# One stage in place of five: input projection, latent up-projections, rotation and bias tables of a two-layer model on one core

## The reference, cut to what matters

```
h = rmsnorm(x, g_attn_norm)                         # 1024 x 1024
proj = h @ w_in                                     # 1024 x 1952
q_a, k_a, v_a, c_q, c_kv, k_rope = split(proj)      # 512, 512, 512, 256, 128, 32 columns
q  = rmsnorm(c_q, g_q_latent) @ w_q_up              # 256 -> 8 heads x (64 + 32)
kv = rmsnorm(c_kv, g_kv_latent) @ w_kv_up           # 128 -> 8 heads x (64 + 64): k_nope, v
q_rope, k_r = apply_rope(q[..., 64:]), apply_rope(k_rope)
bias = rel_bias[bucket(key_pos - query_pos)]        # per head, plus the dilation's log count
```

## Time and profile before

| | us |
|---|---|
| three executions | 5008.50, 5026.09, 5024.47 |
| their median | 5024.47 |
| the profiled execution, its own time | 5014.29 |
| span of its profile | 5012.5 |
| TensorE busy in the span | 4419.9 (88%) |
| VectorE, ScalarE, GpSimd busy | 1840.9, 1680.9, 1239.1 |

### The profile page before, as it was taken

One profiled execution on the slowest core, in us unless ns is written; L12 is line 12 of the kernel. 1 busy time (PEld: TensorE's weight loads), 2 busy tenths in 40 slices (PEclk: granted clock), 3 DMA queues, 4 the chain that ended last, 5 costly groups with the idle time before them and its releaser, 6 DMA issues. The chain is left out here.

```text
span 5012.5 us, 60867 instructions
## 1 busy us (share of the span) xinstructions
PE 4419.9 (88%) x23843; PEld 3654.4 (73%) x23843; DVE 1840.9 (37%) x3384; ACT 1680.9 (34%) x2691; POOL 1239.1 (25%) x646
## 2 busy tenths in 40 slices
PE   7838999767699759999969999949989999999998
PEld 6625999757344347778759999849978877888886
DVE  2122665422111133323136665765522424200154
ACT  2123544310011054553235555534432324211132
POOL 4112322121100023232122332431054211222242
PEclk9966999875799979999979999979989999999999
DMA  3154311233699762232221111121065312322243
GB/s 123 61 159 134 91 43 43 77 120 120 223 325 322 259 217 84 74 102 78 90 84 36 39 52 39 65 68 35 26 225 170 118 59 92 111 74 66 96 152 114
DMA packets 391530, 559.54 MB, mean 112 GB/s; under 512 B 104507, under 2 KB 257723, under 8 KB 389947
## 3 DMA queue, kind: packets, MB, share of 16 engines
q1 hardware_dynamic: 362604, 474.27, 30.1%
q10 hardware_dynamic: 19280, 49.04, 2.5%
q0 software_dynamic: 9376, 32.52, 1.8%
HBM read 402.35 MB, written 153.40 MB: 111 GB/s over the span
## 5 line engine op out<-in xcount | busy, mean ns | idle before, releaser
L2949 POOL TENSOR_TENSOR end_w_lo<-end_w_raw,end_w_hi 128x1024 fp32r<-128x1024 f32 x144 | 353.5, 2463 | 836.0 <-ACT end_w_hi L3138 835.9
L3381 PE MATMUL end_ps<-end_xT_hi,end_w_hi 128*128 128x512 f32 (+1 forms) x896 | 344.7, 385 | 4.7 <-DVE end_xT_lo L2978 2.4
L3381 PE MATMUL end_ps<-end_xT_lo,end_w_hi 128*128 128x512 f32 (+1 forms) x896 | 342.9, 383 | 0.0
L3381 PE MATMUL end_ps<-end_xT_hi,end_w_lo 128*128 128x512 f32 (+1 forms) x896 | 342.8, 383 | 0.0
L1290 PE MATMUL exp_gu_ps<-exp_wgu,exp_xbT 128*128 128x512 f32 x544 | 258.8, 631 | 52.7 <-DMA exp_wgu<-in_w_up 40.4
L2361 POOL TENSOR_TENSOR mid_w_lo<-mid_w_raw,mid_w_hi 128x1024 fp32r<-128x1024 f32 (+1 forms) x64 | 154.2, 2413 | 408.8 <-ACT mid_w_hi L2507 408.8
L662 PE MATMUL att_o_ps<-att_v,att_pT 128*128 128x64 f32 x2048 | 242.6, 272 | 0.0
L1290 PEld LDWEIGHTS exp_gu_ps<-exp_wgu,exp_xbT 128*128 128x128 f32 x544 | 106.9, 202 | 183.3 <-issue 137.6
L3138 ACT ACTIVATE end_w_hi<-end_w_raw 128x1024 fp32r<-128x1024 f32 x144 | 150.0, 1054 | 268.8 <-PE end_ps L3381 139.0
L662 PEld LDWEIGHTS att_o_ps<-att_v,att_pT 128*128 128x128 f32 x2048 | 238.7, 192 | 0.0
L2661 PE MATMUL mid_ps<-mid_w_hi,mid_xT_hi 128*128 128x512 f32 x576 | 229.3, 398 | 6.2 <-DVE mid_xT_lo L2421 6.2
(11 more groups left out here) (576 smaller groups left out, 10450.5 us busy)
## 6 DMA issues: line engine op xcount, KB each, us to landing
exp_wgu<-in_w_gate SPq DMA_DIRECT2D x34, 1024.0 KB, 9.1
exp_wgu<-in_w_up SPq DMA_DIRECT2D x34, 1024.0 KB, 11.6
exp_wd<-in_w_down SPq DMA_DIRECT2D x34, 1024.0 KB, 6.0
mid_w_raw<-in_w_in SPq DMA_DIRECT2D x60, 512.0 KB, 4.0
end_w_raw<-in_w_ffn_in SPq DMA_DIRECT2D x88, 256.0 KB, 3.2
end_w_raw<-in_w_ffn_out SPq DMA_DIRECT2D x44, 512.0 KB, 3.7
expert_rows<-exp_out SPq DMA_DIRECT2D x34, 512.0 KB, 6.3
in_tail<-mid_y SPq DMA_DIRECT2D x56, 256.0 KB, 2.0
```

Of the source, the lines that this page charges most:

```text
L2949: pool.tensor_tensor(halves(w_lo, piece), w_raw[:, 2 * q:2 * q + 2], halves(w_hi, piece).bitcast(F32), ALU.subtract).then_inc(w_split, 1)
L3381: ins = pe.matmul(o_, lhsT, rhs, start=(k == 0 and part == 0), stop=(k == KC - 1 and part == 2))
```

## The change

The five stages become one, `front_layers` "front". What it computes and what the attention reads is the same; q_a, k_a, the table and the latent heads lie in DRAM as before, and v is kept in two tensors of its own (`v_a`, `v_b`).

- The latent columns (chunk "l", 416 columns) are projected first, group by group as the x tiles are turned. The results stay on the chip (`yl`), where ScalarE and VectorE norm them.
- The gains of the norms are folded into the weights as they are split. Weights come in 16 pieces of two K tiles, double-buffered; ScalarE makes the high and VectorE the low parts. GpSimd does nothing but two memsets.
- Then come 24 positions, one group of v, q or k each. Three positions take one latent tile along: its three turns at the first, the product with w_q_up before the second's group and that with w_kv_up in the middle of it, then the rotation, and four batches of four head turns between the halves of the groups that follow. Each batch goes through one PSUM bank and is copied out by ScalarE or VectorE.
- The bias row of all eight heads is made once, by four matmuls of 33 x 8 at the start, and written to DRAM as 8 x 2048. From position 4 on a load spreads one head's row over 128 partitions, and at the next position a store writes it to `skew`.
- Every load and store is issued by SyncE, in one order written out by hand. Groups have two PSUM banks and two buffers of 128 x 512.
- The weights of the up-projections are loaded once all x tiles are turned (their place is that of the x tiles) and split after the last latent tile is kept.

The diff, cut to its core (the bodies of the removed functions are in the section on the kernel before; added lines are moved to the left by eight columns):

```diff
--- before.py
+++ after.py
-def toeplitz_tables(nc, name, rel_bias, onehot_dram, tables, heads, scale):
...
-def head_prep(nc, name, ident_dram, x, kv, dims, cos, sin, outs, gain=None):
...
+FRONT_PLAN = ("l", "v", "q", "k")
+def front_layers(nc, name, a, ident_dram, v_rows, qkT, lat_v, lat_qkT, bias_rows, skew):
...
+    POSITIONS = GROUPS - NT
+    BATCH = 2 * B_HEADS // 4
...
+        def load_piece(n):
+            c, q = divmod(n, PIECES)
+            at, wid = columns(c)
+            if n < 2:
+                sp.wait_ge(hot_done, 4)
+            else:
+                sp.wait_ge(w_split, 2 * (n - 1))
+            src = a["w_in"][2 * q * P:(2 * q + 2) * P, at:at + wid].rearrange("(k p) n -> p k n", p=P)
+            sp.dma_start(w_raw[:, n % 2, :, 0:wid], src).then_inc(w_in[n % 2], 16)
...
+        def load_up():
+            sp.wait_ge(turned, NT)
+            sp.dma_start(raw_q, a["w_q_up"].rearrange("(k p) n -> p k n", p=P)).then_inc(up_in, 16)
+            sp.dma_start(raw_k, a["w_kv_up"]).then_inc(up_in, 16)
...
+        def store_group(G):
+            R = G - NT
+            c, g = divmod(G, NT)
+            taken(sp, G)
...
+        def table_step(m):
+            h, out = divmod(m, 2)
+            if out:
+                sp.wait_ge(rows_in, 16 * (h + 1))
+                sp.dma_start(skew[h].rearrange("(p w) -> p w", w=W), raw[:, 0:W]).then_inc(rows_out, 16)
+            else:
+                if h == 0:
+                    sp.wait_ge(row_out, 16)
+                    sp.wait_ge(up_split, LC)
+                else:
+                    sp.wait_ge(rows_out, 16 * h)
+                sp.dma_start(raw[:, 0:W], bias_rows[h].partition_broadcast(P)).then_inc(rows_in, 16)
...
+        for n in range(2):
+            load_piece(n)
+        sp.dma_start(cs[:], a["rope_cos"].rearrange("(t p) n -> p t n", p=P)).then_inc(turn_in, 16)
+        sp.dma_start(sn[:], a["rope_sin"].rearrange("(t p) n -> p t n", p=P)).then_inc(turn_in, 16)
+        sp.wait_ge(row_kept, 4)
+        sp.dma_start(bias_rows, row8).then_inc(row_out, 16)
+        for n in range(2, PIECES):
+            load_piece(n)
+            load_x(n + 1)
+        for t in range(PIECES + 1, NT):
+            load_x(t)
+            load_piece(t - 1)
+        load_up()
+        load_piece(2 * PIECES - 1)
+        for p in range(POSITIONS + 3):
+            G = NT + p
+            c, g = divmod(G, NT)
+            if p % 3 == 2 and p // 3 < NT:
+                store_values(p // 3)
+            if p % 3 == 0 and p // 3 - 1 in range(NT):
+                store_heads(BATCH * (p // 3 - 1))
+            if p % 3 == 1 and p // 3 - 1 in range(NT):
+                store_heads(BATCH * (p // 3 - 1) + 1)
+                store_heads(BATCH * (p // 3 - 1) + 2)
+            if p % 3 == 2 and p // 3 - 1 in range(NT):
+                store_heads(BATCH * (p // 3 - 1) + 3)
+            if c + 1 < CHUNKS and g % 2:
+                load_piece(PIECES * (c + 1) + g // 2)
+            if 1 <= p <= POSITIONS:
+                store_group(G - 1)
+            if 4 <= p < 4 + 2 * A_HEADS:
+                table_step(p - 4)
...
+        def low_up():
+            dve.wait_ge(up_hi, LC)
+            for k in range(LQ):
+                dve.scalar_tensor_tensor(out=qw_lo[:, k], in0=raw_q[:, k], scalar=gq[:, k:k + 1], in1=qw_hi[:, k].bitcast(F32),
+                                         op0=ALU.mult, op1=ALU.subtract).then_inc(up_split, 1)
+            dve.scalar_tensor_tensor(out=kw_lo[:], in0=raw_k, scalar=gkv[:, 0:1], in1=kw_hi[:].bitcast(F32),
+                                     op0=ALU.mult, op1=ALU.subtract).then_inc(up_split, 1)
...
+        for p in range(POSITIONS + 3):
+            G = NT + p
+            c, g = divmod(G, NT)
+            if p % 3 == 0 and p // 3 - 1 in range(NT):
+                keep_heads(BATCH * (p // 3 - 1) + 1)
+            if p % 3 == 1 and p // 3 - 1 in range(NT):
+                keep_heads(BATCH * (p // 3 - 1) + 3)
+            if 1 <= p <= POSITIONS and (p - 1) % 2:
+                keep_group(G - 1)
+            if p < POSITIONS and p % 3 == 0:
+                low_latents(p // 3)
+            if p < POSITIONS and p % 3 == 1:
+                rotate(p // 3)
+            if c + 1 < CHUNKS and g % 2:
...
+        def keep_latents(t):
+            act.wait_ge(mm_done, t + 1)
+            if t == 0:
+                act.wait_ge(row_out, 16)
+            act.activation(yl[:, t], ps[:, 4 + t % 2, 0:LW], ACT.Copy).then_inc(l_kept, 1)
+            act.wait_ge(l_kept, t + 1)
+            act.activation(scratch[:], yl[:, t, 0:Q_LORA], ACT.Square, scale=Q_LORA ** -0.5, accum_out=cstat[:, 0, t, 0:1]).then_inc(l_squared, 1)
+            act.wait_ge(l_squared, 2 * t + 1)
+            act.activation(scratch[:, 0:KV_LORA], yl[:, t, Q_LORA:Q_LORA + KV_LORA], ACT.Square, scale=KV_LORA ** -0.5,
+                           accum_out=cstat[:, 0, t, 1:2]).then_inc(l_squared, 1)
...
+        def high_up():
+            act.wait_ge(up_in, 32)
+            for k in range(LQ):
+                act.activation(qw_hi[:, k], raw_q[:, k], ACT.Copy, scale=gq[:, k:k + 1]).then_inc(up_hi, 1)
+            act.activation(kw_hi[:], raw_k, ACT.Copy, scale=gkv[:, 0:1]).then_inc(up_hi, 1)
...
+        def keep_up(t):
+            act.wait_ge(q_up, t + 1)
+            if t:
+                act.wait_ge(heads_turned, BATCH * t)
+                act.wait_ge(v_stored, 16 * t)
+            act.activation(mix[:, XS:XS + BANK], ps[:, 1], ACT.Copy).then_inc(q_act, 1)
+            act.wait_ge(kv_up, t + 1)
+            src = ps[:, 3].rearrange("p (h d) -> p h d", d=NOPE + B_DIM)
+            act.activation(ks[:, 0:4, 0:NOPE], src[:, :, 0:NOPE], ACT.Copy).then_inc(kv_act, 1)
...
+        for s in range(NT + 4):
+            if s + 1 < NT:
+                root(s + 1)
+            if s < PIECES:
+                high_weights(s)
+            if 1 <= s <= NT:
+                high_x(s - 1)
+            if 6 <= s < 2 * PIECES + 2:
+                high_weights(s - 2)
+            if s >= 4:
+                keep_latents(s - 4)
+        high_up()
+        for p in range(POSITIONS + 3):
+            G = NT + p
+            c, g = divmod(G, NT)
+            if 1 <= p <= POSITIONS and (p - 1) % 2 == 0:
+                keep_group(G - 1)
+            if p < POSITIONS and p % 3 == 0:
+                high_latents(p // 3)
+            if p % 3 == 0 and p // 3 - 1 in range(NT):
+                keep_heads(BATCH * (p // 3 - 1) + 2)
+            if p < POSITIONS and p % 3 == 1:
+                keep_up(p // 3)
+            if c + 1 < CHUNKS and g % 2:
+                high_weights(PIECES * (c + 1) + g // 2)
+            if p < POSITIONS and p % 3 == 2:
+                keep_heads(BATCH * (p // 3))
...
+        def half_group(G, half):
+            c, g = divmod(G, NT)
+            kind, wid = FRONT_PLAN[c], columns(c)[1]
+            if half == 0:
+                if c == 0:
+                    pe.wait_ge(x_lo, g + 1)
+                if G < 2:
+                    pe.wait_ge(row_kept, 4)
+                elif G < NT + 2 and G - 2 < NT:
+                    pe.wait_ge(l_kept, G - 1)
+                else:
+                    taken(pe, G - 2)
+            for k in range(half * KC // 2, (half + 1) * KC // 2):
+                if g == 0 and k % 2 == 0:
+                    pe.wait_ge(w_split, 2 * (PIECES * c + k // 2 + 1))
+                for part, (xx, ww) in enumerate(((xT_hi, w_hi), (xT_hi, w_lo), (xT_lo, w_hi))):
+                    w = ww[:, c % 2, k]
+                    if kind in "lv":
+                        lhsT, rhs = xx[:, k, g * P:(g + 1) * P], w[:, 0:wid]
+                    else:
+                        j, h = divmod(g, 2)
+                        lhsT, rhs = w[:, j * P:(j + 1) * P], xx[:, k, h * BANK:(h + 1) * BANK]
+                    ins = pe.matmul(ps[:, 4 + G % 2, 0:wid], lhsT, rhs, start=(k == 0 and part == 0), stop=(k == KC - 1 and part == 2))
+            if half:
+                ins.then_inc(mm_done, 1)
...
+        def up_queries(t):
+            pe.wait_ge(c_lo, t + 1)
+            pe.wait_ge(up_split, LC)
+            if t:
+                pe.wait_ge(q_act, t)
+                pe.wait_ge(q_dve, t)
...
+        for g in range(NT):
+            half_group(g, 0)
+            half_group(g, 1)
+            if g + 3 < NT:
+                turn_x(g + 3)
+        for p in range(POSITIONS + 2):
+            late = p // 3 - 1 in range(NT)
+            if p % 3 == 0 and late:
+                turn_heads(BATCH * (p // 3 - 1) + 1)
+            if p % 3 == 1 and late:
+                turn_heads(BATCH * (p // 3 - 1) + 3)
+            if p < POSITIONS:
+                if p % 3 == 0:
+                    turn_latents(p // 3)
+                if p % 3 == 1:
+                    up_queries(p // 3)
+                half_group(NT + p, 0)
+                if p % 3 == 1:
+                    up_keys(p // 3)
+                if p % 3 == 2:
+                    turn_heads(BATCH * (p // 3))
```

(32 more changed lines are left out.)

418 lines of the change are left out of this document (286 added, 132 removed).

## The result

The changed kernel takes 4840.3 us, the median of four executions (4834.7 to 4848.6); with one more execution the kernel before has a median of 5020.4. The ratio is 0.9646, with a 95% interval of 0.962 to 0.9671, so the change makes the kernel 3.5% faster. The forecast was 4847 us in a range of 4815 to 4897. The profiled execution has a span of 4832.8 us and took 4834.7.

The account below looks back on a forecast made before the run. Five front stages ran one behind the other to 435.0 us, mostly waiting or at low clock. The new stage's terms, 31.5 + 36.2 + 4.3 + 175.5 + 4 + 12, sum to 263.5 us, giving 4847 us, range 4815 to 4897.

Parts of the forecast that it names:

- head, to the end of the first group: Start of the new stage: loads, bias row and weight splits end group 0 at 31.5 us, bounds 26 and 38.
- latent groups and x tiles: Seven more groups of latent columns, 31.7 us, and five x tiles to turn, 4.5 us.
- wait for the up-projection weights: TensorE stalls 4.3 us before the first latent tile while ScalarE and VectorE split the up-projection weights.
- v, q, k and latent tiles: 24 groups, 130.6 us, with eight latent tiles between them, 44.9 us: together 175.5 us of TensorE work.
- joints of the tiles: At some of the eight latent-tile joints, late weight pieces cost 4 us in all, bounds 0 and 25.
- tail: After the last group: last heads turned, copied and stored, then the stage change; 12 us, bounds 9 and 18.
- part 5 of the prediction: Bias tables: row-spreading loads and stores replace 32 matmuls of 0.85 us, hidden beside the groups and costed at nothing.
- rival 1: SyncE's single order makes TensorE wait at each of eight latent tiles: 50 us, total 4897 us; chance 0.17.
- Rival 2: Low clock throughout the new stage doubles its TensorE terms: 40 us slower than before, 5058 us; chance 0.02.
- The sign that I had set: Prediction is wrong if the time from 435 us on, behind the front, changes by more than 10 us.

Follow-up runs that it names:

- The experiment on the head: Changed kernel with own tiles for the onehot table and ScalarE's head order changed; stage ends at 258.0 us against 264.9, time 4836.8 us.
- The forced wait: Changed kernel with TensorE made to wait, at each latent tile but the first, until the finished group landed in DRAM; 4886.6 us.
- the doubled tables: Changed kernel with each table load and store done twice, one waiting for the other; stage ends at 315.1 us, time 4896.3 us.
- the tiles behind the groups: Changed kernel with all latent tiles worked after the last of the 24 groups, same instructions; stage ends at 318.0 us, time 4888.9 us.
- the run with the new method alone: Kernel before with only its bias table stage changed to spreading one row by transfers; that stage 80.5 us against 64.7, time 5022.0 us.

## Why the prediction was right

Its reason held: the whole effect is the length of the front, and the new front is TensorE's work plus what cannot be put beside it. By its terms, from the marks shown (the last group ends at 252.0):

| term | predicted | measured |
|---|---|---|
| head, to the end of the first group | 31.5 | 36.3 |
| latent groups and x tiles | 36.2 | 72.4 - 36.3 = 36.1 |
| wait for the up-projection weights | 4.3 | 2.5, and 1.6 of low clock behind it |
| v, q, k and latent tiles | 175.5 | 252.0 - 72.4 - 4.1 - 0.7 = 174.8 |
| joints of the tiles | 4 | 0.7 |
| tail | 12 | 264.9 - 252.0 = 12.9 |
| stage | 263.5 | 264.9 |

**The two terms that were counted from rows of the old trace are right to 0.1 and 0.7 us.** They are 211 of the 265 us: the same matmuls at the same pace, at full clock. The run with the weights split earlier, which has no wait in the second of them, gives 174.4 us for it. This is why the total came out well. That it is off by only 1.4 us is luck in part: the head was 4.8 us and the tail 0.9 us too short, the joints 3.3 us, the counted terms 0.8 us and the wait for the weights 0.2 us too long, and they nearly cancel.

**The head was mis-sized by 4.8 us.** My walk gave the bias row's four matmuls 3.4 us. The trace shows them as eight records in 7.0 us, two for each of these float32 matmuls. The sign stood in the earlier trace rows, where the 32 matmuls of the table stage are counted as 64, and part 5 of the prediction, which spoke of 32 matmuls of 0.85 us, misread it; they are 1.7 us each. The weight pieces stood behind them, issued at 13.8 us. This accounts for 3.6 of the 4.8 us; what the other 1.2 are is open. The experiment on the head took this chain away, together with some of ScalarE's order, and the first group then ended at 29.6.

**The joints cost 0.7 us, and rival 1 did not come.** I had set 4 us for weight pieces that come late. ScalarE did wait for them, three times and 9.6 us in all from 60 us on, but TensorE only once behind it: the 0.7 us at 120 us follow a wait of ScalarE of 4.0 us for a piece, behind which it copied the turned heads. The second profile of the same kernel has not even that one. The forced wait shows that rival 1's price was about right, 5.3 us for each tile against my 6.2, and the doubled tables show that it comes when SyncE is held for 20 us in a pair of positions, longer than the 14.6 us of TensorE's work. The kernel has 5.2 + 5.4 us of landings in them, less than the 8.5 + 3.8 that I counted with; at what length between the two the waits begin no run shows.

**The wait for the weights** came out right in its sum and not in its parts. I gave 4.3 us of waiting; the wait is 2.5 us, and I had left out the low clock behind it. The granted clock is 0.50 from 82 to 84 us and 0.69 in the next two, which loses 2 x 0.50 + 2 x 0.31 = 1.6 us. (The first chunk of the old up-projections, too, was split by ScalarE and VectorE, not by GpSimd; nothing in the sum hangs on it.)

**The tail** was 0.9 us longer. I had set the clearing of more semaphores against a smaller last store. SyncE is done with its own waits at 260.6 us and then waits for the other engines until the next stage starts at 264.9. These are its waits at the ends of stages, first in the changed kernel from 60 to 265 us, then in the kernel before from 250 to 436 us (total, times, longest):

```profile
SPq L85 <- PEq L85: 4.3, 1, 4.3
...
SPq L85 <- PEq L85: 6.6, 4, 2.4
```

The new stage takes 4.3 us for what took the old ones behind the input projection 2.4 us at most. How much of it is the clearing of semaphores no run separates.

**Rival 2**, the low clock throughout, is out: 0.99 from 82 to 250 us. The clock fell after the wait in the middle, after each of the seven forced ones, and in the tiles behind the groups, which ran at 0.76. It did not fall after every wait. In the head of the changed kernel TensorE waits 2.9 us, longer than in the middle, and goes on at full pace:

```profile
35.09 0.45 PE L2447 MATMUL front_ps<-front_w_hi,front_xT_hi 128*128 128x416 f32 x1 [2.90 <-DVE front_w_lo L2214]
...
36.32 1.03 PE L36 MATMUL front_ps<-front_ident,front_mix 128*128 128x128 f32 x8
```

The two further profiles of this kernel show the same, with 2.9 and 3.0 us. In two edited kernels, the one with the forced waits and the one with the weights split earlier, the wait at this place was 3.2 and 3.4 us, and half pace followed. Why a wait of 2.5 us in the middle brought the low clock and one of 2.9 us here did not stays open. The Trainium skill ("TensorE: Matmul & The Clock Gate", section "HAM oscillation — how this bites in real kernels") says of short work between waits for data that every piece starts at the low clock. The forced waits and the tiles behind the groups agree with it, these three waits in the head do not. The rule does not speak against the change, because the groups between the tiles leave TensorE one wait of 0.7 us.

**The rest of the program** is unchanged within its scatter of 17.5 us. The sign that I had set, a change of more than 10 us behind the stage, was finer than this scatter; that it was kept, with 9.6 us, shows little. The forecast was 7 us over the median; 9.6 us of scatter in the profile's favour, 1.4 us too little for the stage and a base set between the runs account for it. The medians differ by 180.1 us in the first comparison and by 166.6 in the later one, on either side of the 170.1 us that the stages give.

## What to carry to other kernels

When several short stages are each bound by a chain of small transfers and copies, count the work that the busiest engine would have if all of them were one stage, at the pace that the trace shows for the same instructions, and add the head and the tail: that sum was right to 1.4 us here, though its counted part alone only to 0.8 and the rest by errors that cancel. A part that is slower by itself (80.5 against 64.7 us for the tables) can still be the right one to put in, if it moves work from the bound engine to a resource that has time; what it has to fit is the time per position of the queue that issues it. And where TensorE, in full work before, waited 2.4 to 4.2 us, it lost 1.6 to 1.8 us more to the clock each time, so a small gap is worth closing.

## What I had not expected

The four matmuls with 8 columns of weights take as long as those with 128 columns did in the old table stage, 1.7 us each: 7.0 us for the four, in the new head as in the table stage of the run with the new method alone, which shows a granted clock of 0.50. A load and a store of 1 MB side by side took 6.5 and 8.5 us to land, where the store alone took 3.8. And the same program varies by 17.5 us in what follows the changed stage, all of it in the expert stage (492.5 and 510.6 us in those two profiles), so a gain of 10 us is seen in the marks of a profile long before it is seen in the times.
